# Two transformer blocks on one core: block 2's tokens in the order of residues mod 16

## The chip, the cores and the metric

The kernel runs on one core of a Trainium2 chip. Its time is that of one launch in device microseconds (us). The engines are named as in the profile: PE is TensorE (matmul), PEld its weight load, DVE VectorE, ACT ScalarE, POOL GpSimd, SP SyncE, which issues most of the DMAs. The kernel before took 2622.14 us, the median of three runs (2611.28 to 2628.56).

## The reference, cut to what matters

x has 2048 tokens of 1024 features. Block 1 (gated spatial mixing, a 31-wide convolution, windowed attention, an output projection with layer norm) gives x1. Block 2 works on x1:

```python
h = rmsnorm(x, norm_pre_g); z = h @ w_in
q, k, v, g_attn, c_h, c_b, c_c, g_conv = split(z)      # q, k, v: 12 heads of 64
q, k = rope(q, pos), rope(k, pos)
for window, dilation in ((128, 1), (512, 4), (2048, 16)):
    # query s sees the keys s, s-d, s-2d, ..., s-window: positions regrouped by
    # residue mod d, then a causal window of 128 keys inside each residue
    o_i, lse_i = dilated_window_attn(q, k, v, window, dilation)
mix_w = softmax(stack(lses)); o = sum(mix_w * outs)    # three patterns mixed per query and head
attn_out = o * silu(g_attn)
conv_out = c_b * causal_depthwise_conv(c_c * c_h, conv_w) * silu(g_conv)   # 3 taps: s, s-1, s-2
x = x + rmsnorm(concat(attn_out, conv_out) @ w_out, norm_post_g)
```

All of it is float32. The kernel forms products from a high and a low part of each operand (three matmuls in the dense projections, L163).

## The kernel before, in words

Block 2 runs in stages: `norm_stage` (x1 rows in from DRAM, normed, transposed, values of all heads), `rope_stage` (q and k), `gate_stage` (gates and convolution), then `dilated_stage`, and in it, after the attention, the output projection. Intermediate tensors go through DRAM (`scr_...`): `q2h`, `q2l`, `k2h`, `k2l` are the high and low parts of q and k, features by tokens; `v23` the values, tokens by heads; `sg2` the gate. `project_stage` before them writes x1, 128 rows at a time (L1325, the last block L1237); `norm_stage` loads it four blocks at a time (L304), each of the first four after the store of just that block.

**Attention.** Heads go in pairs j = 0 to 5. For each pair there are three patterns d = 1, 4, 16 (16, 4, 1 for the last pair), each of 16 units of 128 queries. Unit g is block b of residue r. It sees its own block of 128 keys and the one before it in the same residue (nk = 2, w = 256), or its own alone where there is none before (nk = 1): one unit in d=1, four in d=4, all 16 in d=16. Queries and keys are read from SBUF with stride d.

One unit passes these steps; in the list `work` step s holds scores of unit s, turn and rest of unit s-4, exps of unit s-1, gather of unit s-6, and every engine follows the list in its order:
- scores (PE, L1779 and L1780): for each of the two heads, q's high and low halves (64 + 64 rows) against k's high part twice, and the same against k's low part with zeros in the other half (buffers lA and lB, cleared by POOL once, L1948); both heads in one PSUM bank;
- mask and row maximum (DVE, L1845), exponentials (ACT, L1824);
- turn (PE, L1790): transposes, which ACT (L1817) and DVE (L1851) split into high and low;
- gather (PE, L1808): probabilities times values, ten small matmuls for each key block;
- rows out of PSUM every second unit (DVE L1857 or ACT L1830), into `kept` (d=1) or `ob` (others). Every four units `ob` goes to DRAM (`scr_part`, L1926).

**Mix.** When a pair's third pattern is done, four mixes begin, one for each quarter of the tokens, each in parts A to G on consecutive steps: A (SP, L1936) fetches the two stored patterns' rows into `cm`, and the gate; B (DVE, L1868) is the first use of `cm`; C an exponential (ACT); D, F and G are POOL's (L1731 to L1758), E DVE's. A stands four steps before B; the four A stand 9 steps apart. There are two `cm` buffers, so the third A waits for the first mix's G. SP works through its list in order too: it also holds the loads of the next pair's q and k (L1897 to L1901, ten DMAs of 512 KB, one every second step from unit 8 of d=1 on), the values of the next pattern (L1909, L1913, at unit 6), the part stores. The first pair's q and k come in four chunks of ten DMAs each, and a unit of the first pattern waits for its own chunk alone.

## Time and profile before

| | us |
|---|---|
| median of three runs | 2622.14 |
| profiled execution | 2614.59 |
| its span | 2612.8 |
| PE busy | 2393.4 |
| DVE busy | 1414.2 |
| ACT busy | 840.9 |
| POOL busy | 681.2 |
| share of L163 (dense projections) in the chain that ended last | 50% |

The span runs from the first to the last instruction; the profiled execution's time is 1.8 us more. A busy PE is not PE at its peak: matmuls are pipelined and overlap, so that the distance between the starts of two of them says more than the duration of one. The chain that ended last is followed back from the last instruction, at each step to what released it.

### The profile page before, as it was taken

Reading aid. Unit: us, or ns where it says so; the run is one execution under the profiler, and the core shown is the slowest. Engines: PE = TensorE matmul, PEld = TensorE weight load, DVE = VectorE, ACT = ScalarE, POOL = GpSimd, SP = SyncE. Lnnn points to the kernel's source line nnn. Section 1 sums busy time; section 2 is a strip of 40 time slices with the busy share of each in tenths; the row PEclk is TensorE's granted clock in tenths of the full one; section 3 lists DMA queues with packets and bytes.
Section 4 is the critical chain, followed back from the end, with each engine's and each line's share of the span. In section 5 each row is a group of like instructions: output and inputs, shape, how many; then the busy total and the mean of one; then the engine's idle time right before and its main releaser. Section 6 shows DMA issues by size and latency. Waiting matters only on the chain.

```text
span 2612.8 us, 47838 instructions
## 1 busy us (share of the span) xinstructions
PE 2393.4 (92%) x18958; PEld 2144.8 (82%) x18958; DVE 1414.2 (54%) x3441; ACT 840.9 (32%) x1938; POOL 681.2 (26%) x652
## 2 busy tenths in 40 slices
PE   6999899796999799699999999999699899897898
PEld 5977899796677688599888888889698899896777
DVE  6414768854798454663465533131476676675322
ACT  4411111111567110253122211011475676565111
POOL 0002011153231689200110111110105344443222
PEclk9999899898799899899999999999899999998999
DMA  4341320135640233332455531111858866964442
GB/s 148 113 104 55 102 72 23 58 99 154 178 114 22 101 121 109 121 126 94 143 188 164 175 98 65 49 61 49 200 150 194 204 171 165 203 196 153 147 140 103
DMA packets 283761, 322.19 MB, mean 123 GB/s; under 512 B 38049, under 2 KB 221217, under 8 KB 280081
## 3 DMA queue, kind: packets, MB, share of 16 engines
q1 hardware_dynamic: 281712, 313.09, 41.4%
q0 software_dynamic: 1680, 5.51, 0.7%
q8 instruction: 151, 2.47, 0.4%
q14 instruction: 74, 0.60, 0.1%
q10 hardware_dynamic: 144, 0.52, 0.0%
HBM read 196.91 MB, written 109.56 MB: 117 GB/s over the span
## 4 chain that ended last, share of the span: by engine, by line
PE 67%; DVE 10%; DMA 8%; issue 7%; POOL 3%; SPq 3%; ACT 2%; DVEq 0%; POOLq 0%; ACTq 0%
PE bank L163 50%; DMA cm<-scr_part 4%; PE bank L1779 3%; PE bank L1808 3%; DVE acc L642 3%; PE bank L1780 3%; PE bank L1790 3%; SPq L1899 1%; PE bank L1031 1%; PE bank L352 1%; DMA yn<-scr_y 1%; ACT bf L375 1%; POOL yo L2057 1%; PE bank L1023 1%; DVE bst L312 1%
## 5 line engine op out<-in xcount | busy, mean ns | idle before, releaser
L163 PE MATMUL bank<-w1h,xh 128*128 128x256 f32 (+1 forms) x896 | 260.7, 291 | 15.1 <-DVE s1st L632 15.1
L163 PE MATMUL bank<-w1l,xh 128*128 128x256 f32 (+1 forms) x896 | 256.5, 286 | 0.0
L163 PE MATMUL bank<-w1h,xl 128*128 128x256 f32 (+1 forms) x896 | 256.3, 286 | 0.0
L163 PE MATMUL bank<-xh,w2h 128*128 128x512 f32 x640 | 249.0, 389 | 0.0
L163 PE MATMUL bank<-xl,w2h 128*128 128x512 f32 x640 | 249.0, 389 | 0.0
L163 PE MATMUL bank<-xh,w2l 128*128 128x512 f32 x640 | 249.0, 389 | 0.0
L163 PE MATMUL bank<-w2h,xh 128*128 128x256 f32 x768 | 220.4, 287 | 10.9 <-issue 6.5
L1845 DVE CUSTOM_DVE_ANT_0 s2m<-bank,mask 128x256 f32<-128x256 f32 (+1 forms) x576 | 186.6, 362 | 72.0 <-PE bank L1780 68.4
L163 PE MATMUL bank<-w2h,xl 128*128 128x256 f32 x768 | 219.7, 286 | 0.0
L163 PE MATMUL bank<-w2l,xh 128*128 128x256 f32 x768 | 219.6, 286 | 0.0
L642 DVE SCALAR_TENSOR_TENSOR acc<-ain,cw,acc 128x512 f32<-128x512 f32 x240 | 200.3, 836 | 8.9 <-ACT acc L599 1.8
L163 PEld LDWEIGHTS bank<-w1h,xh 128*128 128x128 f32 x896 | 176.5, 197 | 18.6 <-issue 17.6
L1851 DVE SCALAR_TENSOR_TENSOR p2l<-bank,p2h 128x512 f16<-128x512 f32 (+1 forms) x288 | 165.1, 573 | 46.9 <-ACT p2h L1817 35.6
L1817 ACT ACTIVATE p2h<-bank 128x512 f16<-128x512 f32 (+1 forms) x288 | 144.8, 503 | 128.1 <-PE bank L1790 126.2
L1790 PE MATMUL bank<-ident,p2r 128*128 128x128 f32 x900 | 154.8, 284 | 31.7 <-DVE p2l L1851 31.7
L163 PEld LDWEIGHTS bank<-w1l,xh 128*128 128x128 f32 x896 | 176.4, 197 | 1.6 <-issue 0.6
L163 PEld LDWEIGHTS bank<-w1h,xl 128*128 128x128 f32 x896 | 176.0, 196 | 0.0
L1808 PE MATMUL bank<-v,p2h 128*128 128x64 bf16 (+1 forms) x2700 | 169.2, 194 | 0.8 <-issue 0.5
L1808 PEld LDWEIGHTS bank<-v,p2h 128*128 128x128 f16 x2700 | 160.3, 98 | 4.3 <-issue 0.4
L163 PEld LDWEIGHTS bank<-w2h,xh 128*128 128x128 f32 x768 | 149.6, 195 | 12.0 <-issue 6.7
L1808 PE MATMUL bank<-v,p2l 128*128 128x64 bf16 (+1 forms) x1800 | 158.8, 194 | 0.0
L213 POOL CAST w2h<-w2r 128x2048 fp32r<-128x2048 f32 x13 | 24.6, 1895 | 509.5 <-DMA w2r<-in_w_in 411.0
(256 smaller groups left out, 6215.6 us busy)
## 6 DMA issues: line engine op xcount, KB each, us to landing
v<-scr_v SPq DMA_DIRECT2D x12, 1552.0 KB, 9.7
scr_part<-ob SPq DMA_DIRECT2D x48, 264.0 KB, 3.2
cm<-scr_part SPq DMA_DIRECT2D x48, 264.0 KB, 4.6
w2r<-in_w_in SPq DMA_DIRECT2D x12, 1024.0 KB, 6.2
qr<-qf SPq DMA_DIRECT2D x192, 64.0 KB, 2.0
scr_v<-bvo SPq DMA_DIRECT2D x24, 388.0 KB, 2.5
v<-scr_v SPq DMA_DIRECT2D x24, 388.0 KB, 5.8
ax<-in_x SPq DMA_DIRECT2D x16, 512.0 KB, 6.3
```

Of the source, the lines that this page charges most:

```text
L163: ins = nc.tensor.matmul(dst, x, y, start=k == 0 and m == 0, stop=k == n - 1 and m == 2)
L312: nc.vector.bn_stats(st[:, t, 6 * h:6 * h + 6], xs[t][:, 512 * h:512 * h + 512]).then_inc(*d_st.up())
L352: ins = nc.tensor.transpose(bank[:, 128 * t:128 * t + 128], xs[t][:, 128 * k:128 * k + 128], ident[:])
L375: nc.scalar.activation(xf[m % 2][:], bank[:], ACT.Identity, scale=gain[:, k:k + 1], **bias).then_inc(*a_turn.up())
L642: nc.vector.scalar_tensor_tensor(acc[:, cols], ain[:, 512 * q + m:512 * q + m + 512], cw[:, c, m:m + 1], acc[:, cols], ALU.mult, ALU.add). ...
L1779: nc.tensor.matmul(dst, buf[hh][:, qc], buf[2 + hh][:, kc], start=True, stop=False)
L1780: ins = nc.tensor.matmul(dst, buf[hh][:, qc], buf[4 + hh][:, kc], start=False, stop=True)
L1790: ins = nc.tensor.transpose(bank[:, w * hh + 128 * c:w * hh + 128 * c + 128], p[:, hh, 128 * c:128 * c + 128], ident[:])
L1808: ins = nc.tensor.matmul(bank[:, c0:c0 + n], a[:, pc], vt[:, x["v0"] + c, vc], start=c == 0 and m == 0, stop=c == nk - 1 and m == 4)
L1817: nc.scalar.activation(pth[u % 3][:, 0:2 * x["w"]], x["t"][0][:, 0:2 * x["w"]], ACT.Copy, scale=PSCALE).then_inc(*a_ph.up())
L1845: nc.vector.tensor_tensor_reduce(sm[u % 3][:, hh, 0:w], x["s"][0][:, 256 * hh:256 * hh + w], mask2[:, 256 - w:256], 1.0, -NEG, ALU.add, AL ...
L1851: nc.vector.scalar_tensor_tensor(ptl[u % 3][:, 0:w], x["t"][0][:, 0:w], PSCALE, pth[u % 3][:, 0:w], ALU.mult, ALU.subtract).then_inc(*d_pl ...
```

## The change

Block 2 takes its tokens in the order of residues mod 16: position 128 r + l holds token 16 l + r. x1 is stored so, and every later tensor of block 2 has this order; the output rows go back to their places at the last store. In it the keys of a d=16 unit are 128 neighbours; those of a d=4 block are 4 runs of 32; those of a d=1 block 16 runs of 8 (`blocks`). Inside a unit, queries, keys, values and mask have the order of these runs.

- x1's row blocks are stored as 8 x 16 rows (`x1_rows`), and block 2's first load waits for all of them.
- Rope reads cos and sin with a stride of 16. The convolution's taps are 128 columns apart, with one more small copy on DVE.
- The patterns' order is 16, 4, 1 (1, 4, 16 for the last pair). `kept` holds d=16; d=4 and d=1 go to DRAM.
- For d=4 and d=1 POOL copies the queries of four units at a time into `qd` (item "reorder", one copy per head, 128x512), 6 to 8 steps ahead.
- k's low part has one buffer: head 0 in rows 0 to 63, head 1 in rows 64 to 127. The matmul with it takes 64 rows. The zero fills go.
- Two units are scored at once, each head in a bank of its own. Of each unit: high of both heads, then low of both.
- Values and parts move by residue: 1 DMA for d=16, 4 for d=4, 16 for d=1 (`STRIPES`, 8 d partitions each). A pattern's rows are stored in one go when all 16 units are done.
- Masks for d=4 and d=1 are loaded by 4 and 16 DMAs at the stage's start and reordered by DVE.
- A mix's A stands 9 steps before its B, and the four A 7 steps apart, the first 3 steps later than before.

```diff
+STRIPES = {1: 16, 4: 4, 16: 1}
...
-                elif x_ready is not None:
-                    sp.wait_ge(*x_ready[t])
+                elif t == 0:
+                    for token in x_ready:
+                        sp.wait_ge(*token)
...
+        def x1_rows(n):
+
+            return x1.rearrange("(r t l) c -> t l r c", r=16, t=NT)[n]
...
-        return [(x_out[t], x_out[t].base + 16) for t in range(4)]
+        return [s.now() for s in (*x_out, x_last)]
...
-                c, q, r = x["c"], qf[m % 3], qr[m % 2]
+                q, r = (b[:].rearrange("p (r l) -> p r l", r=4) for b in (qf[m % 3], qr[m % 2]))
+                cos, sin = (b[:].rearrange("p (l r) -> p r l", r=16)[:, 4 * x["g"]:4 * x["g"] + 4, :] for b in (cosT, sinT))
                 dve.wait_ge(*a_q.at(m + 1))
                 dve.wait_ge(*r_in[m % 2].at(64 * (m // 2 + 1)))
                 dve.wait_ge(*c_in.at(32))
-                nc.vector.tensor_tensor(q[:], q[:], cosT[:, c:c + 512], ALU.mult).then_inc(*d_rp.up())
-                nc.vector.tensor_tensor(r[:], r[:], sinT[:, c:c + 512], ALU.mult).then_inc(*d_rp.up())
+                nc.vector.tensor_tensor(q, q, cos, ALU.mult).then_inc(*d_rp.up())
...
+                        nc.vector.tensor_copy(uin[:, 0:2, 1:128], uin[:, 16:18, 0:127]).then_inc(*d_z.up())
...
+        part_rows = sbs("prow", 2, [128, NT, PW], F32, late_scope)
...
-        qk = [[sb(f"qk{n}{i}", [128, S], FR, scope) for n in ("qA", "qB", "kA", "kB", "lA", "lB")] for i in range(2)]
+        qk = [[sb(f"qk{n}{i}", [128, S], FR, scope) for n in ("qA", "qB", "kA", "kB", "l")] for i in range(2)]
+        qd = [sbs(f"qd{i}", 2, [128, 4, 128], FR, scope) for i in range(3)]
         vr = sbs("v2", 2, [128, 16, 2 * VW], BF, scope)
-        ob = sbs("ob", 4, [128, 4, PW], F32, scope)
         sm, pr = sbs("s2m", 3, [128, 2, 256], F32, scope), sbs("p2r", 4, [128, 2, 256], F32, scope)
         pth, ptl = sbs("p2h", 3, [128, 512], FH, scope), sbs("p2l", 3, [128, 512], FH, scope)
-        mask2 = sb("mask2", [128, 256], scope=scope)
-
-        m_in, qk_in, q0_in, v_in, o_out = sem("ld0"), sems("qk", 2), sems("qk0", 4), sems("v2", 2), sems("ob", 4)
+        mask = {d: sb(f"mask{d}", [128, 256], scope=scope) for d in PATTERNS}
...
-        pairs = [(j, d) for j in range(6) for d in (PATTERNS if j < 5 else PATTERNS[::-1])]
+        d_mx, d_pl, d_row, d_min, d_rec, d_mix, d_mask = (sem("d_" + n) for n in ("mx", "pl", "row", "min", "rec", "mix", "mask"))
+        g_q, g_mix = sem("g_q"), sem("g_mix")
+
+        ORDER = PATTERNS[::-1]
+        pairs = [(j, d) for j in range(6) for d in (ORDER if j < 5 else ORDER[::-1])]
...
+        fours = [u for u in range(0, N, 4) if units[u]["d"] < 16]
+        for n, u in enumerate(fours):
+            for x in units[u:u + 4]:
+                x["of4"] = n
...
-            mixing.append([t, [None] * delay + ["A"] + [None] * (3 if j < 5 else 0) + list("BCDEFG")])
+            mixing.append([t, [None] * delay + ["A"] + [None] * (8 if j < 5 else 0) + list("BCDEFG")])
...
-                if g == 15 and d == 16 and j < 5:
+                if g == 15 and d == 1 and j < 5:
                     for quarter in range(4):
-                        mix(j, quarter, quarter == 3, 9 * quarter, "pool", work)
-                if j == 5 and d == 1 and g % 4 == 3:
+                        mix(j, quarter, quarter == 3, 3 + 7 * quarter, "pool", work)
+                if j == 5 and d == 16 and g % 4 == 3:
...
+            if s % 2 == 0 and s - s % 4 + 8 in fours:
+                work.append(("reorder", s - s % 4 + 8, s % 4 // 2))
+            if g == 7 and d == 16:
                 loading = [("pair", j + 1, 1, k) for k in range(10)] if j + 1 < 6 else []
             if (j, d, g) == (5, 4, 0):
                 work += [("weights", 0), ("weights", 1)]
-            if (g + 16 * PATTERNS.index(d) if d < 16 else 0) >= 8 and g % 2 == 0 and loading:
+            if (g + 16 * ORDER.index(d) if d > 1 else 0) >= 8 and g % 2 == 0 and loading:
                 work.append(loading.pop(0))
...
-                x["s"] = sbk.take(d_mx.at(2 * item[1] + 2))
-                if x["d"] > 1:
-                    if x["g"] % 4 == 0:
-                        n_ob += 1
+
+                u = item[1]
+                x["s"] = [banks[u // 2 % 2 * 2 + hh][:, 256 * (u % 2):256 * (u % 2) + x["w"]] for hh in range(2)]
+                x["s_before"] = s_before if u < 4 else [d_mx.at(2 * (u - 4) + 4)]
...
+        def blocks(x, d):
+
+            return x.rearrange("p (r t l) -> p t r l", t=NT, l=8 * d)
+
+        def stripes(x, d):
+
+            return x.rearrange("(r t l) c -> r l t c", t=NT, l=8 * d)
...
-            if item[0] == "scores":
-                u, x = item[1], units[item[1]]
-                j, d, w, buf = x["j"], x["d"], x["w"], qk[x["j"] % 2]
-                bank, before = x["s"]
+            if item[0] == "scores" and item[1] % 2 == 0:
+                two = units[item[1]:item[1] + 2]
+                x = two[1]
+                j, d, buf = x["j"], x["d"], qk[x["j"] % 2]
                 if j == 0:
-                    for c in range(x["g"] // 4 + 1 if d == 1 else 4):
+                    for c in range(x["g"] // 4 + 1 if d == 16 else 4):
                         pe.wait_ge(*q0_in[c].at(160))
                 else:
                     pe.wait_ge(*qk_in[j % 2].at(160 * ((j + 1) // 2)))
-                pe.wait_ge(*g_zero.at(4))
-                pe.wait_ge(*before)
-                q0, k0 = x["r"] + d * 128 * x["b"], x["r"] + d * 128 * (x["b"] - x["nk"] + 1)
-                qc, kc = slice(q0, q0 + d * 127 + 1, d), slice(k0, k0 + d * (w - 1) + 1, d)
-                for hh in range(2):
-                    dst = bank[:, 256 * hh:256 * hh + w]
-                    nc.tensor.matmul(dst, buf[hh][:, qc], buf[2 + hh][:, kc], start=True, stop=False)
-                    ins = nc.tensor.matmul(dst, buf[hh][:, qc], buf[4 + hh][:, kc], start=False, stop=True)
-                ins.then_inc(*p_s.up())
+                if d < 16:
+                    pe.wait_ge(*g_q.at(2 * (x["of4"] + 1)))
+                for before in two[0]["s_before"]:
+                    pe.wait_ge(*before)
+                for x in two:
+                    for second in (False, True):
+                        for hh in range(2):
+                            g, k0 = x["g"], x["g"] - x["nk"] + 1
+                            dst = x["s"][hh].rearrange("p (t r l) -> p t r l", t=x["nk"], l=8 * d)
+                            q = buf[hh][:, 128 * g:128 * g + 128] if d == 16 else qd[x["of4"] % 3][hh][:, g % 4, :]
+                            own = slice(64 * hh, 64 * hh + 64)
+                            if second:
+                                ins = nc.tensor.matmul(dst, q[own], blocks(buf[4][:], d)[own, k0:g + 1], start=False, stop=True)
+                            else:
+                                nc.tensor.matmul(dst, q, blocks(buf[2 + hh][:], d)[:, k0:g + 1], start=True, stop=False)
+                ins.then_inc(*p_s.up(2))
...
+            if item[0] == "reorder":
+                _, u, hh = item
+                x = units[u]
+                j, d, g, n = x["j"], x["d"], x["g"], x["of4"]
+                if n >= 3:
+                    pool.wait_ge(*p_s.at(fours[n - 3] + 4))
+                for token in [q.at(160) for q in q0_in] if j == 0 else [qk_in[j % 2].at(160 * ((j + 1) // 2))]:
+                    pool.wait_ge(*token)
+                nc.gpsimd.tensor_copy(qd[n % 3][hh][:].rearrange("p t (r l) -> p t r l", l=8 * d), blocks(qk[j % 2][hh][:], d)[:, g:g + 4]).then_inc(*g_q.up())
...
-                nb, c = NT // d, 2 * VW * j
+                c = 2 * VW * j
                 if n >= 2:
                     sp.wait_ge(*p_o.at(16 * (n - 1)))
-                if d == 16:
-                    nc.sync.dma_start(vr[n % 2][:], v23.rearrange("(p r) c -> p r c", r=16)[:, :, c:c + 2 * VW]).then_inc(*v_in[n % 2].up(16))
-                else:
-                    view = v23.rearrange("(b p r) c -> r p b c", p=128, r=d)
-                    for r in range(d):
-                        nc.sync.dma_start(vr[n % 2][:, r * nb:r * nb + nb, :], view[r][:, :, c:c + 2 * VW]).then_inc(*v_in[n % 2].up(16))
+                for r in range(STRIPES[d]):
+                    nc.sync.dma_start(vr[n % 2][8 * d * r:8 * d * r + 8 * d, :, :], stripes(v23[:, c:c + 2 * VW], d)[r]).then_inc(*v_in[n % 2].up(16))
...
-                if g % 4 == 3 and d > 1:
-                    p = part[PATTERNS.index(d) - 1][j]
-                    dst = (p.rearrange("(b p r) c -> r p b c", p=128, r=4)[g // 4] if d == 4 else
-                           p.rearrange("(p r) c -> p r c", r=16)[:, g - 3:g + 1, :])
+                if g == 15 and d < 16:
                     for token in x["rows"]:
                         sp.wait_ge(*token)
                     sp.wait_ge(*d_mx.at(2 * u + 2))
-                    nc.sync.dma_start(dst, ob[x["ob"] % 4][:]).then_inc(*o_out[x["ob"] % 4].up(16))
+                    for r in range(STRIPES[d]):
+                        nc.sync.dma_start(stripes(part[d][j], d)[r], out_of(x)[8 * d * r:8 * d * r + 8 * d, :, :]).then_inc(*o_out[x["ob"] % 2].up(16))
...
-                for i in range(4):
-                    sp.wait_ge(*o_out[i].at(16 * (2 * j + 2)))
+                for token in parts_at[j]:
+                    sp.wait_ge(*token)
                 if k >= 2:
                     sp.wait_ge(*after[mix_order[k - 2], "G"])
-                for n in range(2):
-                    nc.sync.dma_start(cm[slot][:, :, n, :], part[n][j][rows, :].rearrange("(t p) c -> p t c", p=128)).then_inc(*cm_in[slot].up(16))
+                for n, d in enumerate((4, 1)):
+                    nc.sync.dma_start(cm[slot][:, :, n, :], part[d][j][rows, :].rearrange("(t p) c -> p t c", p=128)).then_inc(*cm_in[slot].up(16))
...
-        def pool_zeros():
-            for buf in qk:
-                for hh in range(2):
-                    nc.gpsimd.memset(f(buf[4 + hh][64 - 64 * hh:128 - 64 * hh, :]), 0.0).then_inc(*g_zero.up())
-
-        nc.sync.dma_start(mask2[:], A["c_mask2"]).then_inc(*m_in.up(16))
-        pool_zeros()
+
+        nc.sync.dma_start(mask[16][:], A["c_mask2"]).then_inc(*m_in.up(16))
+        for d in (4, 1):
+            for r in range(STRIPES[d]):
+                nc.sync.dma_start(sm[d // 4][8 * d * r:8 * d * r + 8 * d, 0, :], A["c_mask2"].rearrange("(l r) k -> r l k", r=STRIPES[d])[r]).then_inc(*m_in.up(16))
+        dve.wait_ge(*m_in.at(16 * 21))
+        for d in (4, 1):
+            nc.vector.tensor_copy(mask[d][:].rearrange("p (t r l) -> p t r l", t=2, l=8 * d),
+                                  sm[d // 4][:, 0, :].rearrange("p (t l r) -> p t r l", t=2, l=8 * d)).then_inc(*d_mask.up())
...
-                    nc.sync.dma_start(out_dst[128 * n:128 * n + 128, :], ybuf[n % 3][:]).then_inc(*o2_out[n % 3].up(16))
+                    nc.sync.dma_start(out_dst.rearrange("(l r) c -> r l c", r=16)[n], ybuf[n % 3][:]).then_inc(*o2_out[n % 3].up(16))
...
```

## Rows read from the trace of the kernel before

**Rows 1.** The page's chain that ended last: shares by engine, then by line.

```profile
PE 67%; DVE 10%; DMA 8%; issue 7%; POOL 3%; SPq 3%; ACT 2%; DVEq 0%; POOLq 0%; ACTq 0%
PE bank L163 50%; DMA cm<-scr_part 4%; PE bank L1779 3%; PE bank L1808 3%; DVE acc L642 3%; PE bank L1780 3%; PE bank L1790 3%; SPq L1899 1%; PE bank L1031 1%; PE bank L352 1%; DMA yn<-scr_y 1%; ACT bf L375 1%; POOL yo L2057 1%; PE bank L1023 1%; DVE bst L312 1%
```

**Rows 2.** By stretch: length, busy PE PEld DVE ACT POOL (instructions), clock, DMA share, GB/s.

```profile
2031.00:2120.00 89.00, 82.13 (x1092) 80.31 (x1091) 61.86 (x269) 59.47 (x157) 39.62 (x76) 0.98 0.78 187
...
2210.00:2302.00 92.00, 84.82 (x1093) 83.22 (x1091) 62.54 (x272) 59.35 (x156) 39.65 (x76) 0.94 0.76 181
2302.00:2385.00 83.00, 76.81 (x1081) 75.21 (x1080) 64.92 (x259) 58.23 (x152) 49.59 (x95) 1.00 0.58 169
```

**Rows 3.** Timeline of PE, a d=1 unit: start us, us, instruction.

```profile
2034.33 0.36 PE L1779 MATMUL bank<-qkkA,qkqA 128*128 128x256 f32 x1
2034.54 0.28 PE L1780 MATMUL bank<-qklA,qkqA 128*128 128x256 f32 x1
...
2034.89 0.60 PE L1790 MATMUL bank<-ident,p2r 128*128 128x128 f32 x4
...
2035.93 0.36 PE L1779 MATMUL bank<-qkkA,qkqA 128*128 128x256 f32 x1
```

**Rows 4.** Timeline of PE, scores of a d=4 unit.

```profile
1973.84 0.58 PE L1779 MATMUL bank<-qkkA,qkqA 128*128 128x256 f32 x1
...
1974.96 0.29 PE L1790 MATMUL bank<-ident,p2r 128*128 128x128 f32 x1
```

**Rows 5.** Timeline of PE, scores of a d=16 unit.

```profile
2103.83 0.44 PE L1779 MATMUL bank<-qkkA,qkqA 128*128 128x128 f32 x1
...
2104.74 0.40 PE L1790 MATMUL bank<-ident,p2r 128*128 128x128 f32 x2
```

**Rows 6.** Timeline of PE in the window stage of block 1.

```profile
700.49 0.42 PE L1022 MATMUL bank<-kTA,qTA 128*128 128x384 f32 x1
700.83 0.44 PE L1023 MATMUL bank<-kTl,qTA 64*128 64x384 f32 x1
701.20 0.55 PE L1031 MATMUL bank<-ident,pr 128*128 128x128 f32 x3
```

**Rows 7.** Waits, 1853 to 2302 us: total, times, longest.

```profile
DVE ce L1868 <- DMA cm<-scr_part: 51.1, 12, 8.5
...
PE bank L1790 <- DVE p2l L1851: 26.4, 10, 5.7
```

**Rows 8.** Timeline of PE at the start of the attention, idle before in brackets.

```profile
1859.27 0.58 PE L1779 MATMUL bank<-qkkA,qkqA 128*128 128x256 f32 x1 [10.34 <-DMA qklB<-scr_k2l]
```

**Rows 9.** Timeline at the last x1 store (DVE, ACT) and at attention's start (SP).

```profile
1073.67 1.28 DVE L312 BATCH_NORM_STATS2 bst<-bx 128x6 f32<-128x512 f32 x2
...
1073.79 0.34 ACTq L1237 DMA_DIRECT2D scr_x<-xr  x1
...
1835.65 0.35 SPq L1950 DMA_DIRECT2D mask<-in_c_mask  x1
...
1836.06 0.49 SPq L1899 DMA_DIRECT2D qkqA<-scr_q2h  x1
```

**Rows 10.** DMA issues: KB each, median us from issue to landing.

```profile
v<-scr_v SPq DMA_DIRECT2D x12, 1552.0 KB, 9.7
...
cm<-scr_part SPq DMA_DIRECT2D x48, 264.0 KB, 4.6
...
bx<-scr_x SPq DMA_DIRECT2D x16, 512.0 KB, 5.8
...
scr_x<-xr SPq DMA_DIRECT2D x15, 512.0 KB, 3.0
```

**Rows 11.** POOL's instructions by line: busy us, mean ns.

```profile
L1750 POOL TENSOR_TENSOR cm<-cm,cd 128x512 f32<-128x512 f32 x42 | 43.0, 1045 | 0.0
...
L1754 POOL TENSOR_TENSOR kept<-kept,cm 128x512 f32<-128x512 f32 x21 | 27.1, 1288 | 1.6
...
L213 POOL CAST w2h<-w2r 128x2048 fp32r<-128x2048 f32 x13 | 24.6, 1895 | 509.5 <-DMA w2r<-in_w_in 411.0 <-PE bank L163 49.3 <-DMA qr<-qf 49.1
```

75 lines of the change are left out of this document (44 added, 31 removed).

## The prediction

> **What bounds the kernel now.** I read the page's chain first, then the busy time by stretches, then the instructions one by one. The chain [rows 1] is two thirds TensorE; half is the dense projections (L163), which the change leaves alone but for the order of the tokens. What changes lies in block 2's dilated attention, 1836 to about 2385 us. I cut it by head pair (48 units each; the five with mixes are like one another but for the last): 89 to 92 us per pair, in which TensorE is busy 82 to 85, DVE 62, ACT 59, POOL 40, and the DMA engines 0.76 to 0.78 of the time, so about 69 us of full DMA work per pair [rows 2]. TensorE is the bound, DMA close behind. The last pair loads nothing for a next one: 83 us, DMA at 0.58.
>
> What TensorE does in one unit of two key blocks with d=1: scores from 2034.33 to 2034.89, 0.56 us; turning and gathering last until 2035.93: 1.60 together [rows 3]. With d=4 the same four score matmuls take 1.12 (1973.84 to 1974.96) [rows 4], and with d=16, where a unit has 128 keys, 0.91 [rows 5]. So the reader sees the strides: half the columns with d=16 cost 1.6 times as much as d=1. A pair is 16 d=1 units (one of them with one key block), 16 d=4 (four with one), 16 d=16 (all with one).
>
> The second loss is waits. Between 1853 and 2302 DVE waited 51.1 us in 12 places for the mix's data from DRAM (cm), and TensorE in its turn 26.4 us for DVE [rows 7], some 6.6 per pair with mixes.
>
> **The change part by part.**
>
> Scores. The keys become runs of 8 or 32 elements, d=16 queries a plain block, others are copied by POOL: the strides go. But the low part becomes a 64-row matmul where it was a 128-row one with zeros, and the order in a unit is high, high, low, low: two switches of row shape per unit. What a switch costs is seen in the window stage, whose scores are built so: the 128-row matmul of 384 columns starts at 700.49, the 64-row one at 700.83, the next 128-row one at 701.20 [rows 6], steps of 0.34 and 0.37, where [rows 3] has 0.12 (2034.54 to 2034.89 in three) for 256 columns without a switch. The rows leave 0.21 between first and second matmul after a gather (a weight load laid bare, 0.10 above that pitch). My unit of two key blocks: 0.21 (high to high) + 0.19 (0.34 less that 0.10, less 0.05 for 128 fewer columns) + 0.05 (second low, between nothing, if the two run beside each other on their own rows, and 0.11) + 0.32 (0.37 less 0.05) = 0.77 us; with one key block 0.10 less, 0.67. Bounds: 0.45 if no switch costs anything and the lows overlap (0.56 less 0.11); 0.93 if every step costs as in [rows 6].
>
> The Trainium skill (TensorEngine Tiling (Array Packing), Key Properties) says both that different tiles can load and multiply in parallel and that changing the tiling mode drains the TensorE. By its first sentence alone the unit would be at my lower bound; the second is what [rows 6] show, and I go by the row.
>
> Per pair: d=1 15 x (+0.21) + 0.11 = +3.3; d=4 12 x (0.77 - 1.12) = -4.2, 4 x (0.67 - 0.91) = -1.0; d=16 16 x (0.67 - 0.91) = -3.8. Sum -5.7, six pairs -34. In the first pair the gain of the first pattern is not had: its 16 units wait for their four chunks of q and k (TensorE idle 10.34 us before 1859.27 [rows 8]; ten issues of 0.6 us per chunk), +4. So **-30**.
>
> Scoring two units at once only changes who waits within two units: both engines behind have spare time (DVE 62, ACT 59 of about 77 [rows 2]). Nothing.
>
> Later mixes. From the issue of cm to its first use there are 9 steps instead of 4, at 1.6 us about 14 us instead of 7, against 4.6 us landing when quiet [rows 10]. But cm still queues behind the loads of the next pair and now behind 16 value loads and 16 part stores on SP; a part store is also only issued when its pattern is done. And the third mix's fetch waits for the first one's G (7 us of POOL: three products of 1.05, three further operations of 1.29 [rows 11]) in SP's order, with the values of d=1 and three q/k loads queued behind it, then the fourth mix's fetch. I leave 3 of the 6.6 us: four pairs x 3.6 = **-14**. Bounds: -26 (all gone), +15 (as much lost again at the fourth mix).
>
> POOL gets 96 copies of 128x512. Between a quarter of the 2048-wide cast (0.47) and a two-input operation (1.29) [rows 11]; I take 0.7: 11 us a pair on top of 40, hidden by TensorE's 77. They stand 6 to 8 units ahead, about 10 us, and G's 7 us can stand before them: no stall, little room. Upper bound 1 us a pair.
>
> DMA issues. SP issues 63 in a pair against 36; the smallest cost 0.35 each [rows 9]. 22 us of SP's time is hidden. Not hidden: at the stage's start 20 small mask loads go ahead of the first q load, which now is issued at 1836.06, right after one mask load of 0.35 to 0.41 [rows 9]. 20 x 0.4 = **+8**, nothing covers it, for TensorE waits for exactly these loads. The two mask reorderings on DVE lie under the same wait. The four zero fills on POOL go, hidden before.
>
> x1. Block 2's first four loads (512 KB each) needed only the first four row blocks and had landed before the last was stored; now they need all rows. The last store is issued at 1073.79 [rows 9], lands 3.0 later, the first load 5.8 after that [rows 10]: the statistics of the norm, which began at 1073.67 [rows 9], begin at about 1082.6. TensorE waits for them: **+9** (7 to 13).
>
> Rope with strided cos/sin, one small copy per convolution half, output rows 64 KB apart in DRAM: rope and gates stand in the chain with the projections' L163 [rows 1], DVE beside it; output rows stay 4 KB pieces. Nothing. If that cover were gone: 96 strided rope operations, at 0.1 us more each 10 us.
>
> The last pair has no loads for a following one; its mixes still use their data at once. Nothing.
>
> Sum: -30 - 14 + 8 + 9 = **-27**. The profiled execution took 2614.6 us (span 2612.8), so 2588; the median of three is 7.5 above it. Between the two scales I say 2590.
>
> **The rivals.**
>
> A. The switches cost little, the low matmuls run side by side: 0.45 per unit. Then TensorE loses 19.5 us a pair (d=1 16 x 0.11, d=4 12 x 0.67 + 4 x 0.48, d=16 16 x 0.48 with 0.43 for one block) and has about 63 and no longer bounds; DMA does, with 69 us of work [rows 2]. At some 75 us per pair instead of 89: four pairs x -14.5, -8 in the last, -4 in the first, -70, +17 for the starts: -53, 2562. For it: the two lows go to different rows and banks. Against it: [rows 6]. 0.25.
>
> B. Slower: the d=1 values and parts move as 16 pieces of 8 partitions. If such a piece keeps only 8 of the 16 DMA engines busy, those eight carry 1.55 MB of values [rows 10] and 1.08 MB of parts (2048 rows of 528 bytes) twice as long. A pair moves 187 GB/s x 89 us = 16.6 MB in 69 us of DMA work [rows 2], 4.2 us a MB: 69 + 11 = 80 us on the busier half, more than TensorE's 77 (82.7 - 5.7). cm, values and q/k of the next pair then land late, each before an engine that stops for it: 10 us in each of five pairs, -27 + 50 = +23, 2638. It decides where these eight engines need more than the pair's TensorE time. No row has a transfer of fewer than 32 partitions to judge by, so 0.16.
>
> The Trainium skill (DMA: Bandwidth & Descriptors, Why a DMA increments its semaphore by 16 and not by 1) says the number of engines is the largest up to 16 that divides both sides' slowest dimension: 8 here. No row here shows it; it speaks for B, and for 2 us more at x1.
>
> C. It doesn't pay: the switch from high to low costs 0.29, the 0.10 of [rows 6] not taken off: 0.87 per unit, +0.10 x 48 = +4.8 a pair, +27 in all: 0, 2614 to 2622. At 0.93 it is +17, 2632 to 2639. 0.14.
>
> The forecast's own case 0.45, 2565 to 2605.
>
> **How the numbers follow.** This kernel's measurement tells about 1% (26 us) from no change; the forecast lies right on it. Faster by over 1%: 0.27 of the forecast's 0.45 and all of A: 0.52. Within: 0.18, and 0.12 of C: 0.30. Slower: B and the rest, 0.18. The range 2550 to 2635 leaves out a tenth at A's end (copies and waits all hidden) and a tenth at B's.
>
> **What would show it.** In the profile after: the steps of the score matmuls in one d=1 unit (0.77 us for four; 0.45 would be A, 0.87 C); weight loads of q shorter than now; idle before 64-row matmuls put to "issue"; DVE's wait for cm under 25 us; POOL's copies near 0.7; the first score matmul some 8 us later after the last gate store; 9 us more between the last x1 store and the first transpose; time from issue to landing of the d=1 values and the DMA share per pair (B). Wrong if a pair takes under 73 or over 88 us.

## The result and the profile after

| | us | |
|---|---|---|
| before, median of 4 beside it | 2620.1 | 2611.3 to 2628.6 |
| changed, median of 4 | 2767.5 | 2759.2 to 2775.2 |
| ratio | 1.0562 | [1.0512, 1.0613] |
| profiled execution, span (mean clock) | 2760.7 (0.917) | before: 2612.8 (0.956) |

147 us slower where 27 us faster was forecast. The chain of waits of the changed kernel, shares by engine and by line:

```profile
PE 61%; DMA 11%; DVE 9%; issue 8%; SPq 5%; POOL 4%; ACT 2%; DVEq 0%; POOLq 0%; ACTq 0%
PE bank L164 48%; DMA cm<-scr_part 6%; DVE acc L644 3%; PE bank L1857 3%; PE bank L1839 3%; SPq L1978 2%; PE bank L1829 2%; PE bank L1827 1%; DMA scr_part<-prow 1%; PE bank L1033 1%; PE bank L354 1%; ACT bf L377 1%; PE bank L1025 1%; SPq L1957 1%; SPq L1988 1%
```

Against [rows 1] TensorE's share falls from 67% to 61%, and DMA rises from 8% to 11%, SP's queue from 3% to 5%; the line of the part stores (L1978) is new in it. The projections (L164 now) are the same work. I date each part of the attention by its first unit's eviction of p2l, 48 units to a pair:

| us | first p2l | pair 1 | 2 | 3 | 4 | 5 | 6 | from last p2l to the end |
|---|---|---|---|---|---|---|---|---|
| before | 1861.4 | 81.3 | 88.3 | 89.3 | 90.3 | 91.6 | 80.5 | 230.0 |
| changed | 1876.8 | 92.1 | 116.6 | 119.5 | 115.3 | 114.5 | 98.2 | 227.9 |

So 15.4 us are lost ahead of the attention, 134.7 in it, and 2.2 come back behind it. These are dates of one execution each: in the kernels of e1, e3, e4, e6, e10 and e13, which change nothing ahead of the attention, the first p2l comes anywhere from 1875.7 to 1884.9. The busy time in three of these pairs (columns in the first line, as in [rows 2]):

```profile
core 0: us, PE busy (x) PEld busy (x) DVE busy (x) ACT busy (x) POOL busy (x), PEclk, DMA share, GB/s
1968.90:2085.40 116.50, 85.91 (x1096) 72.68 (x1093) 62.52 (x268) 58.40 (x157) 48.78 (x92) 0.81 0.76 143
2085.40:2204.90 119.50, 84.58 (x1099) 71.52 (x1096) 62.33 (x268) 58.47 (x158) 48.62 (x92) 0.81 0.75 139
...
2434.70:2532.90 98.20, 79.67 (x1074) 68.38 (x1071) 62.03 (x254) 56.59 (x152) 54.18 (x103) 0.85 0.60 149
```

TensorE is busy for 86 us of 116.5, and so idle for 30; before it was busy for 82 of 89. It is busy for longer although the strides are gone: its clock is 0.81 where [rows 2] have 0.98 to 0.94. (The clock has two levels, 1.00 is 2.4 GHz and 0.50 is 1.2 GHz; a value between is the mean of a stretch.) Two stretches, the first inside an idle stretch of TensorE, the second right behind it:

```profile
1991.00:1998.00 7.00, 0.00 (x0) 0.00 (x0) 1.09 (x7) 0.11 (x1) 0.67 (x4) 0.50 1.19 220
1999.00:2007.00 8.00, 8.00 (x72) 6.92 (x71) 5.81 (x24) 4.92 (x13) 7.00 (x12) 0.50 1.03 200
```

TensorE stands idle for over 9 us eight times in the four middle pairs. Each time the clock goes to its lower level during the idle stretch and stays there past its end. The bytes are the same (143 GB/s x 116.5 us = 16.7 MB), but the DMA engines work 0.76 x 116.5 = 88 us on them, not 69. (The share adds up the times of all packets over 16 engines; packets overlap, so it can come out above 1.) The waits (total us, times, longest) say what TensorE stands idle for:

```profile
DVE ce L1917 <- DMA cm<-scr_part: 156.8, 16, 21.5
...
PE bank L1839 <- DVE p2l L1900: 95.8, 18, 13.5
...
PE bank L1857 <- issue: 46.3, 5, 13.0
```

DVE's wait for the mix's data is 156.8 us; before it was 58.1 up to the stage's end (51.1 of it in the stretch of [rows 7]), and its longest grew from 8.5 to 21.5. DVE's evictions queue behind it, and TensorE's wait for them went from 31.7 (26.4 of it in [rows 7]) to 95.8. The 46.3 us ahead of the gathers (L1857), put to "issue", are waits for the values: in the four middle pairs TensorE stands 9.3 to 13.0 us ahead of the gather of the first d=1 unit, and where the values come in one DMA (e2, below) 0.6 is left. Yet TensorE's own pace is as forecast. Timeline of PE, the scores of two d=1 units (start, us, instruction):

```profile
2069.01 0.38 PE L1829 MATMUL bank<-qkkA,qd 128*128 128x256 f32 x1
2069.22 0.30 PE L1829 MATMUL bank<-qkkB,qd 128*128 128x256 f32 x1
2069.45 0.40 PE L1827 MATMUL bank<-qkl,qd 64*128 64x256 f32 x2
2069.79 0.40 PE L1829 MATMUL bank<-qkkA,qd 128*128 128x256 f32 x1
2070.02 0.30 PE L1829 MATMUL bank<-qkkB,qd 128*128 128x256 f32 x1
2070.25 0.40 PE L1827 MATMUL bank<-qkl,qd 64*128 64x256 f32 x2
2070.58 0.66 PE L1839 MATMUL bank<-ident,p2r 128*128 128x128 f32 x4
```

Eight score matmuls take 2069.01 to 2070.58: 0.785 us a unit, forecast 0.77. The two low matmuls, one row "x2", share 0.40 us: their two records start within 0.01 us of each other and take 0.40 each, so they run side by side. What went wrong stands in the timeline of SP's queue (start, time that the issues took, tensor, count):

```profile
1970.59 11.58 SPq L1978 DMA_DIRECT2D scr_part<-prow  x16
1982.21 2.70 SPq L1967 DMA_DIRECT2D v<-scr_v  x4
1985.34 3.19 SPq L1988 DMA_DIRECT2D cm<-scr_part  x2
...
2008.70 0.92 SPq L1988 DMA_DIRECT2D cm<-scr_part  x2
2019.97 0.36 SPq L1991 DMA_DIRECT2D gt<-scr_sg  x1
2020.37 13.26 SPq L1967 DMA_DIRECT2D v<-scr_v  x16
2033.67 0.86 SPq L1957 DMA_DIRECT2D qkqB<-scr_q2h  x1
...
2035.85 3.34 SPq L1988 DMA_DIRECT2D cm<-scr_part  x2
```

Sixteen part stores take 11.6 us to issue, 0.72 each, sixteen values 13.3, 0.83 each. The first cm fetch stands behind the stores and four value loads of d=4; the fourth behind the sixteen values and three q/k loads. The place in the queue isn't all: the fourth fetch begins to be issued at 2035.85, and DVE's wait for it, 21 us, ends at 2058.8, 23 us later ([rows 10] has 4.6 from issue to landing).

### The profile page after: what moved, and what is told of

It is laid out like the page before. It is cut to its first block, busy times and chain, and to the rows that moved or that the text cites. A ratio compares the mean times of both kernels' runs of the same rounds, so it can differ in the third digit from the quotient of the medians.

```text
span 2760.7 us, 48109 instructions
## 1 busy us (share of the span) xinstructions
PE 2414.8 (87%) x18958; PEld 2095.6 (76%) x18958; DVE 1460.8 (53%) x3445; ACT 830.5 (30%) x1938; POOL 721.6 (26%) x744
## 4 chain that ended last, share of the span: by engine, by line
PE 61%; DMA 11%; DVE 9%; issue 8%; SPq 5%; POOL 4%; ACT 2%; DVEq 0%; POOLq 0%; ACTq 0%
PE bank L164 48%; DMA cm<-scr_part 6%; DVE acc L644 3%; PE bank L1857 3%; PE bank L1839 3%; SPq L1978 2%; PE bank L1829 2%; PE bank L1827 1%; DMA scr_part<-prow 1%; PE bank L1033 1%; PE bank L354 1%; ACT bf L377 1%; PE bank L1025 1%; SPq L1957 1%; SPq L1988 1%
## 5 line engine op out<-in xcount | busy, mean ns | idle before, releaser
L164 PE MATMUL bank<-w1h,xh 128*128 128x256 f32 (+1 forms) x896 | 260.2, 290 | 14.9 <-DVE s1st L634 14.9
L1839 PE MATMUL bank<-ident,p2r 128*128 128x128 f32 x900 | 180.9, 318 | 99.9 <-DVE p2l L1900 95.8
L164 PE MATMUL bank<-w1l,xh 128*128 128x256 f32 (+1 forms) x896 | 256.2, 286 | 0.0
L164 PE MATMUL bank<-w1h,xl 128*128 128x256 f32 (+1 forms) x896 | 256.1, 286 | 0.0
L164 PE MATMUL bank<-xh,w2h 128*128 128x512 f32 x640 | 249.0, 389 | 0.0
L164 PE MATMUL bank<-xl,w2h 128*128 128x512 f32 x640 | 249.0, 389 | 0.0
L164 PE MATMUL bank<-xh,w2l 128*128 128x512 f32 x640 | 249.0, 389 | 0.0
L1857 PE MATMUL bank<-v,p2h 128*128 128x64 bf16 (+1 forms) x2700 | 188.7, 204 | 46.3 <-issue 46.3
L164 PE MATMUL bank<-w2h,xh 128*128 128x256 f32 x768 | 220.5, 287 | 9.7 <-issue 6.4
L164 PE MATMUL bank<-w2l,xh 128*128 128x256 f32 x768 | 219.7, 286 | 0.0
L164 PE MATMUL bank<-w2h,xl 128*128 128x256 f32 x768 | 219.6, 286 | 0.0
L1857 PEld LDWEIGHTS bank<-v,p2h 128*128 128x128 f16 x2700 | 177.3, 106 | 53.6 <-issue 47.2
L1839 PEld LDWEIGHTS bank<-ident,p2r 128*128 128x128 f32 x900 | 106.6, 157 | 119.8 <-DVE p2l L1900 98.5
L164 PEld LDWEIGHTS bank<-w1h,xh 128*128 128x128 f32 x896 | 176.3, 197 | 18.4 <-issue 17.4
L164 PEld LDWEIGHTS bank<-w1l,xh 128*128 128x128 f32 x896 | 175.9, 196 | 1.6 <-issue 0.6
L1857 PE MATMUL bank<-v,p2l 128*128 128x64 bf16 (+1 forms) x1800 | 176.2, 203 | 0.0
L164 PEld LDWEIGHTS bank<-w1h,xl 128*128 128x128 f32 x896 | 175.8, 196 | 0.0
L1873 ACT ACTIVATE p2r<-s2m,prow 128x256 f32<-128x256 f32 (+1 forms) x384 | 165.9, 483 | 0.0
```

Source lines behind the costliest of these rows:

```text
L164: ins = nc.tensor.matmul(dst, x, y, start=k == 0 and m == 0, stop=k == n - 1 and m == 2)
L1839: ins = nc.tensor.transpose(bank[:, w * hh + 128 * c:w * hh + 128 * c + 128], p[:, hh, 128 * c:128 * c + 128], ident[:])
L1857: ins = nc.tensor.matmul(bank[:, c0:c0 + n], a[:, pc], vt[:, x["v0"] + c, vc], start=c == 0 and m == 0, stop=c == nk - 1 and m == 4)
L1873: nc.scalar.activation(pr[u % 4][:, hh, 0:w], sm[u % 3][:, hh, 0:w], ACT.Exp, bias=row[:, 130 + hh:131 + hh], scale=-1.0).then_inc(*a_ex.up())
```

## The experiments

The theories. **Pieces**: the 16 small DMAs of d=1 cost the time, through the engines that they keep busy (rival B) or through SP's time and order. **Switches**: the row switches cost TensorE more than the strides did. **Mix places**: the later mixes lose time rather than win it. **Gate**: a gate fetch that waits in SP's queue for a slot's y store holds back what stands behind it. In the expectations "theory S" is the width of the pieces, "theory I" the issues, "theory Q" SP held by the mix's own waits, for a free cm buffer and for the gate's store. All ratios are to the kernel before on the same chip; a difference between two kernels is the difference of their ratios times 2618.

### e1, e13: the same sixteen DMAs, other partitions

```diff
-    for r in range(16): dma(vr[8*r:8*r+8, :, :], stripes(v, 1)[r])         # 8 partitions x 16 tiles
+    for t in range(16): dma(vr[:, t, :], v.rearrange("(r t l) c -> t r l c", t=16, l=8)[t])   # e1: 128 partitions x 1 tile
+    for r in range(16): dma(vr[16*(r//2):16*(r//2)+16, 8*(r%2):8*(r%2)+8, :], plain(v)[same])  # e13: 16 partitions x 8 tiles
```

(The part stores alike. e13 moves plain rows, so it attends to other tokens; only its time counts.)

> The changed kernel, but the values and parts of d=1 still move in 16 DMAs, each now over all 128 partitions (one tile of 128 rows) instead of 8 partitions and 16 tiles; same bytes, same pieces of 776 and 528 bytes, same number of issues. Theory S (pieces of 8 partitions load only part of the DMA engines, so the transfers take longer and all behind them is late): the mix's wait for cm falls from 151 us to under 70, the kernel comes to 2640 to 2700. Theory I (the price is the 16 issues in SP's order, 11 to 13 us each time): nothing changes in the issues, 2750 to 2780. Theory Q (SP is held by the mix's own waits for a free buffer and for the gate store): 2740 to 2780.

e1: 2699.0 us (2686.8 to 2705.0), 1.0308 [1.0268, 1.0349]. Its waits:

```profile
DVE ce L1917 <- DMA cm<-scr_part: 97.9, 16, 11.5
...
PE bank L1839 <- DVE p2l L1900: 87.9, 17, 10.5
```

The waits fell with the time, though not under the 70 us that theory S wanted: 66 us (0.0254) come from the form of the pieces at the same number of them. e1 changes the number of partitions from 8 to 128, though, and could win by the span of partitions or by the number of engines. e13 tells these apart.

> The changed kernel, with the values and the stored parts of d=1 again in 16 DMAs each, but each of 16 partitions by 8 tiles and not of 8 partitions by 16 tiles (plain rows, so other tokens are attended to; bytes, number of issues and their places are the same). If the number of DMA engines that serve a piece of 8 partitions is what made the changed kernel dearer than e1_spread (rival B's mechanism): near e1_spread, 2690 to 2715 us, and the waits of the mixes for cm near e1's 98 us. If it is that a piece covers few partitions: near the changed kernel, 2745 to 2775 us, and those waits near 151 us.

e13: 2700.2 us (2694.0 to 2701.6), 1.0306 [1.0278, 1.0334]. For the kernel's time pieces of 16 partitions are as good as pieces of 128, and both 66 to 67 us better than pieces of 8. Stretches in which the part stores, then the values, move (last columns: DMA share, GB/s), first of the changed kernel, then of e13 with one of its pairs, then of e1:

```profile
1972.00:1984.00 12.00, 12.00 (x168) 10.34 (x165) 10.51 (x56) 9.12 (x32) 0.00 (x0) 1.00 0.45 90
2024.00:2032.00 8.00, 6.33 (x56) 4.91 (x54) 4.40 (x17) 4.12 (x11) 6.53 (x19) 0.79 0.62 99
```

```profile
1973.00:1981.00 8.00, 8.00 (x120) 7.07 (x119) 6.89 (x39) 6.22 (x21) 0.00 (x0) 1.00 0.75 126
2020.00:2027.00 7.00, 7.00 (x92) 5.78 (x90) 4.83 (x20) 4.48 (x12) 5.95 (x9) 0.89 1.06 134
2072.50:2170.70 98.20, 82.30 (x1099) 69.37 (x1096) 62.23 (x268) 58.33 (x158) 48.60 (x92) 0.88 0.85 169
```

```profile
1974.00:1985.00 11.00, 11.00 (x157) 9.61 (x154) 9.61 (x54) 8.59 (x29) 0.00 (x0) 1.00 0.37 94
2026.00:2035.00 9.00, 7.34 (x103) 5.83 (x102) 6.22 (x26) 5.52 (x15) 7.44 (x19) 1.00 0.70 190
```

While the stores move, the share is 0.45 in the changed kernel, with 8-partition pieces, and 0.75 with 16; while the values move 0.62 (a y store moves beside them) and 1.06. The share alone doesn't tell how many engines a piece uses: e1, with all 128 partitions, has 0.37 and 0.70. The DMA packets in the trace do. In the changed kernel 8 to 11 value packets (776 bytes) are under way at once for nine tenths of 2022 to 2032; in e13 it is 16 or more for over three quarters of 2020 to 2027. e13's pair takes 98.2 us instead of 119.5. The sixteen issues of e13, then of e1 (0.51 and 0.54 us each in e13, 0.69 in e1, where the changed kernel has 0.72 and 0.83):

```profile
1972.28 8.20 SPq L1984 DMA_DIRECT2D scr_part<-prow  x16
...
2018.48 8.62 SPq L1968 DMA_DIRECT2D v<-scr_v  x16
```

```profile
1973.36 10.97 SPq L1983 DMA_DIRECT2D scr_part<-prow  x16
...
2024.81 10.99 SPq L1968 DMA_DIRECT2D v<-scr_v  x16
```

So SP's long issues are not simply the engines' backlog: e1's take 0.69 us each while the DMA share is 0.37. What makes an issue long stays open. Rival B's mechanism is shown: an 8-partition piece keeps half of the 16 engines busy. With the rule of the Trainium skill that the prediction quoted (DMA: Bandwidth & Descriptors, Why a DMA increments its semaphore by 16 and not by 1), 8 engines at 8 partitions and 16 at 16, the trace agrees: 8 to 11 packets under way against 16 and more.

A second cost lies in few partitions with many tiles. Over the attention the median packet of 776 bytes takes 62 ns in the changed kernel and 65 in e13, but 38 in e1, in e2 and in the kernel before. So the DMA work of a pair grows (88 us; e13 0.85 x 98.2 = 83) also where all 16 engines serve a piece. e13's transfers are slower than e1's and its issues shorter, so the two equal times may be a balance of both; no run parts them.

### e2, e6, e7: no pieces at all

```diff
-    for r in range(16): dma(vr[8*r:8*r+8], stripes(v, d)[r])
+    dma(vr[:], v.rearrange("(t p) c -> p t c", p=128))        # e2, e6; part stores alike in e2 alone
-    matmul(dst, q[own], k_low[own])                            # e7: e2 and this
+    matmul(dst, q, k_low)
```

> The changed kernel, but every pattern's values and parts move in one DMA each, rows in plain order (so the values and parts of d=4 and d=1 are of other tokens than they should be; times alone are of use). 1 issue instead of 16 and 4. Theory S and I both: a large fall; what it gains over the run with 16 DMAs of 128 partitions is the price of the issues. S alone: like that run, 2640 to 2700. I alone: 2620 to 2660, while that run stays near 2767. Theory Q: still over 2700, since the third mix's fetch still holds SP.

(e2, e6 and e7 read other tokens' rows, and e7 also adds products that don't belong; only their times count.)

e2: 2621.6 us (2617.5 to 2629.0), 1.0021 [1.0006, 1.0037]. Its waits and two of its pairs:

```profile
DVE ce L1917 <- DMA cm<-scr_part: 35.7, 12, 7.0
...
PE bank L1839 <- DVE p2l L1900: 32.1, 12, 5.9
```

```profile
2048.00:2130.00 82.00, 79.06 (x1097) 66.92 (x1094) 62.42 (x269) 57.95 (x157) 48.78 (x92) 0.94 0.85 203
2130.00:2214.30 84.30, 78.17 (x1097) 66.05 (x1094) 61.85 (x268) 58.23 (x157) 48.65 (x92) 0.96 0.84 197
```

142 us (0.0541) came from the form of the values' and parts' transfers and nothing else: bytes, tensors, waits and places in the queue are the same. e2 also makes one DMA of the four pieces of d=4; no run parts these from the sixteen of d=1. The clock is back at 0.94 and 0.96 with TensorE fed, and its busy time per pair falls from 86 to 79 us. So what the rest of the change wins it also loses.

> The changed kernel with its values in one DMA per pattern, rows in plain order (values of d=4 and d=1 are of other tokens; times alone are of use); parts still in 4 and 16 pieces. Both in one DMA each came to 2622, none to 2767. If the values are the dearer part (they stand between the third and the fourth mix's fetch): 2665 to 2690. If the parts are (the first mix's fetch waits for their landing): 2700 to 2735.

e6: 2653.2 us (2651.3 to 2667.2), 1.0146 [1.0104, 1.0188]. It came below both ranges expected. The values carry 109 us of the 142, the stores 33. The values stand just ahead of the q/k loads and the fourth mix's fetch.

> The run with one DMA for each pattern's values and parts (2622 us, other tokens' rows), and the low matmul over all 128 rows (products of a low q part with the other head's low k part are added). With the waits gone TensorE's pace should decide more than in the changed kernel, where the 128 rows brought 31 us: 2575 to 2590. If the DMA engines bound it, under 15 us: 2607 to 2622.

e7: 2595.8 us (2587.0 to 2602.9), 0.9911 [0.9875, 0.9946], the fastest of all, but no version to use. It came between the two ranges expected. The 64-row form costs 0.0110, 29 us give or take 10, where the pieces are not in the way.

### e3: the low part without the row switch

```diff
-    matmul(dst, q[own], k_low[own], start=False)      # 64 rows
+    matmul(dst, q, k_low, start=False)                # 128 rows
```

> The changed kernel, but the matmul with k's low part takes all 128 rows (it adds products of the other head that don't belong; times alone are of use): no switch of row shape. The scores of two units should take about 1.1 us instead of 1.57 when nothing else waits. If TensorE's pace sets the time, some 0.2 us x 288 = 60 us less, 2700 to 2715; if the waits for data do, under 20 us, 2745 to 2770.

e3: 2736.3 us (2732.4 to 2740.4), 1.0457 [1.0427, 1.0487]: 27 us less than the changed kernel, between the two ranges expected, though DVE waits longer for cm (176.1, where it was 156.8). The switches are real and small: 27 us, give or take some 15, of a loss of 147 plus a missed gain of 27.

### e4: the mixes at their old places

```diff
-  ["A"] + [None] * (8 if j < 5 else 0)      mix(..., 3 + 7 * quarter, ...)
+  ["A"] + [None] * (3 if j < 5 else 0)      mix(..., 9 * quarter, ...)
```

> The changed kernel with the mixes' old places: A 4 steps before B and 9 steps apart, first A at once. If the later mixes help as meant, 20 to 50 us more than 2767. Theory Q (the buffer wait that the new places bring, third A before the first mix's G is done, holds SP with the values behind it): equal or less, 2720 to 2770.

e4: 2794.9 us (2785.4 to 2796.3), 1.0683 [1.0649, 1.0717]. The later mixes help, by 32 us: the rival that they hurt falls.

### e5: the pieces spread over the steps

```diff
+    if 6 <= g < 14: work += two ("value", n + 1, t)            # instead of 16 in a row
-    if g == 15: 16 part stores
+    if g % 2 == 1: the part stores of the two units just done   # pieces as in e1
```

> The run with 16 DMAs of 128 partitions for d=1's values and parts (2699 us), but spread in SP's order: two value loads on each of eight steps instead of sixteen in one step, two part stores after every second unit instead of sixteen when the pattern is done. Same DMAs, same sizes, same number. If what remains of the loss is that 16 issues in a row stand before the mix's fetch and the next loads (theory I, order): 2620 to 2655, DVE's wait for cm under 60 us. If it is the number of DMAs as such (each takes its time on the engines or in SP wherever it stands): 2680 to 2705.

e5: 2660.5 us (2656.5 to 2663.8), 1.0162 [1.0127, 1.0197]: 38 us less than e1 with the same DMAs. DVE's wait for cm is 47.1 us, its longest 6.0 instead of 11.5. The time lies between its two cases. What is left to e2 is 37 us: the number of DMAs, that of d=4 with it, and their places. TensorE still waits 20.5 us ahead of the gathers, for values that now come step by step (e2: 0.6), so not all of the 37 is the number itself.

### e8, e9, e12, e14: a better version of the change

```diff
e8:  e5 + e3's 128-row low + the masks as three plain loads behind the first q/k chunk
e9:  e8 + gate fetch (gt) moved on SP from the mix's part A to its part B
e12: e9 + mix starts 3 + 9 * quarter (were 3 + 7 * quarter)
e14: e9 + the d=1 value loads on ACT's queue (were on SP's)
```

> Spread issues, low matmul over all 128 rows, and the three masks as three plain loads behind the first chunk of q and k instead of 21 DMAs ahead of it. The terms as they stand: the run with spread issues less 30 us (rows), less 8 (masks): 2580 to 2620, at best 1% under the kernel before. If SP's issues as such are the price, 2640 to 2665.

e8: 2618.3 us (2610.6 to 2621.4), 0.9998 [0.998, 1.0017]: no gain over the kernel before. With the 128-row low matmul e8 and the three built on it add to each score the product of q's low part with the other head's low k part, which the reference doesn't have.

> The same move of the gate's fetch on the run with spread issues, 128-row low matmul and plain masks (2618 us). Its SP stood 12.6 us between the third mix's cm and gate fetch. If values and q/k behind it come earlier for it: 2585 to 2605. If the DMA engines (share 0.84 over a pair) are the bound by now: 2610 to 2620.

e9: 2610.8 us (2608.2 to 2619.1), 0.9973 [0.9959, 0.9987]: 7 us under e8, no more than the two intervals can tell. One of its pairs:

```profile
2040.80:2124.50 83.70, 71.73 (x1099) 69.88 (x1095) 61.94 (x269) 57.77 (x157) 48.61 (x92) 0.90 0.91 198
```

TensorE needs 72 us and the pair takes 84, with the DMA engines at 0.91. They are nearer to a bound than TensorE is, but no run shows that they are the bound: TensorE's waits for DVE still add up to 52.0 us.

> As the one before, and the mixes' four starts 9 steps apart instead of 7, so that the third fetch finds its cm buffer free (or nearly). If SP's hold there (some 7 us a pair) counts: 10 to 20 us less than with 7 steps. If the last mix, now 6 steps later, collides with the next pair's loads instead: equal or up to 15 more.

e12: 2633.2 us (2630.1 to 2640.7), 1.0061 [1.0041, 1.0081]: 23 us worse than e9 (at most 15 were expected), with DVE's wait for cm at 78.6 us. Mixes further apart don't help. Its waits show where they hurt: TensorE stands 21.9 us ahead of the gathers (4.3 in e9), and DVE waits 24.7 us for POOL's last step of a mix.

> e9_gate with the value loads of d=1 issued from ACT's queue, at the same steps, and no longer from SP. If SP's time for issues is still what holds the mixes' fetches: 2595 to 2606 us, and DVE's wait for cm falls from 38.5 to under 20 us. If the transfers' own time is: 2608 to 2620 us with that wait as it is. A third case: ACT's issues (some 0.7 us each, 16 per pair, by the SP rows) delay its evictions and exps; then PE's wait for p2h and p2l rises and the time is 2620 to 2660 us.

e14: 2635.8 us (2630.7 to 2643.0), 1.0055 [1.0029, 1.0081]: 21 us worse than e9. Waits of e9, then of e14 (TensorE's wait for DVE goes from 52.0 to 59.3):

```profile
DVE p2l L1902 <- ACT p2h L1868: 68.9, 78, 6.9
...
DVE ce L1919 <- DMA cm<-scr_part: 38.5, 11, 6.3
```

```profile
DVE p2l L1908 <- ACT p2h L1868: 93.6, 87, 10.1
...
DVE ce L1925 <- DMA cm<-scr_part: 38.1, 11, 6.0
```

The wait for cm doesn't move when SP is freed of 16 issues a pair: SP's time is no longer what holds the mixes back. ACT's evictions come later (93.6 against 68.9), the expectation's third case.

### e10: the gate fetch alone

> The changed kernel with one edit: the gate's fetch for a mix stands in SP's order beside part B instead of part A, nine steps later, when its buffer has long been stored. Theory Q (SP held about 10 us a pair by the wait for the gate store, the 16 value loads behind it): 30 to 50 us less than 2767. If that hold is only shifted to the next wait, under 15 us.

e10 (e9's move of the gate fetch, made on the changed kernel): 2788.4 us (2780.2 to 2800.4), 1.0653 [1.062, 1.0687], 24 us slower than the changed kernel, where both cases had it faster.

```profile
PE bank L1839 <- DVE p2l L1900: 162.8, 15, 24.6
...
POOL gt L1800 <- DMA gt<-scr_sg: 123.0, 9, 24.5
...
DVE ce L1917 <- DMA cm<-scr_part: 73.0, 11, 14.3
```

The wait for cm halves (from 156.8), and yet TensorE waits 162.8 for DVE, where it was 95.8: the wait only moved to a place where it hurts more. It is the same mechanism with another load: the second mix's gate fetch now stands behind the sixteen values (issued at 2035.34), POOL waits 123.0 us for the gate in nine places, ACT's exponential for POOL, and the evictions for ACT. So moving the gate fetch alone is no cure, and the total of one wait doesn't order two kernels.

### e11: the kernel before with the later mixes

e4's diff turned round, made on the kernel before, with e9's gate fetch.

> The kernel before (old order of tokens, strided keys) with two edits: A nine steps before B, starts 3, 10, 17, 24 steps after the pattern's end as in the changed kernel, and the gate's fetch beside B. If the later mixes were the useful part of the change: 20 to 30 us less than before, 2585 to 2600 (26 us of TensorE's waits are there to be had). If they only help where the DMAs are late: within 8 us of before.

e11: 2601.7 us (2599.1 to 2606.6), 0.9939 [0.9922, 0.9955]: the best version, faster than both kernels. Its waits, then a pair in the middle and the last:

```profile
PE bank L1790 <- DVE p2l L1851: 11.3, 5, 5.4
...
DVE ce L1868 <- DMA cm<-scr_part: 6.6, 2, 6.3
```

```profile
2033.60:2115.90 82.30, 81.30 (x1099) 79.85 (x1095) 63.04 (x271) 59.74 (x157) 39.76 (x76) 1.00 0.82 202
2281.00:2368.50 87.50, 78.37 (x1046) 76.77 (x1047) 63.77 (x255) 57.51 (x151) 49.61 (x95) 0.94 0.55 160
```

The wait for cm is 6.6 us (58.1 in the kernel before), and a pair takes 82.3 us with the clock at 1.00: TensorE is busy for 81.3 of it. The gain of 16 us lies between the two cases expected. It is that of the later places and of the gate fetch together.

## Why the prediction was wrong, step by step

**The step that failed** is the term DMA issues, which the sum put at nothing: "22 us of SP's time is hidden", at "the smallest cost 0.35 each". Measured were 0.72 and 0.83 us each, and they were not hidden. The next cm fetches stood in line behind them (DVE waited 156.8 us for cm, TensorE 95.8 for DVE), and the values themselves came late (46.3 us of TensorE's). I took the smallest price, counted the total, and never asked which load stands behind sixteen issues in a row; that the transfers themselves get slower was left to rival B. Of the 142 us that e2 gave back, 66 are the pieces' form (e1, e13), 38 their standing in a row (e5), 37 their number, with that of d=4 and what the spread places leave (e2 against e5), each give or take 10 to 17 by the intervals. These follow one another in that order; another order of the edits may divide the sum otherwise. Why such an issue takes 0.7 us and not 0.35 stays open.

**Rival B** had the mechanism right, and the chance (0.16) and price (+50) wrong. It counted 11 us more work for the busier half and 10 us per pair; the four middle pairs grew by 27 each (116.5 against 89.9 in the mean). The sum took DMA work at 4.2 us a MB; it was 88 / 16.7 = 5.3, for the single packets take longer as well, which "the busier half works longer" doesn't contain. That growth isn't what the 66 us bought: e13 has most of it (83 us of work a pair) and is as fast as e1. And rival B held one load late for one wait, where each late cm stops DVE, DVE stops TensorE, and TensorE then runs at a clock of 0.81: 86 us busy for what takes 79 in e2. That last step, what TensorE loses at the lower level of its clock, was nowhere in the prediction.

**Scores** (-30): the unit was right, 0.785 for 0.77. Rival C (0.87) and A (0.45) are out. Its worth shows only in e2, and only at the same clock: at 0.94 TensorE is busy for 79.1 us a pair where [rows 2] have 84.8, so -5.8 where -5.7 was forecast. The low matmul's switches cost 27 to 29 us of what the removed strides give.

**Later mixes** (-14, bounds -26 to +15): -32 in the changed kernel (e4), with the queue fuller; on the kernel before, together with the gate fetch, -16 (e11). My worry about the gate's slot isn't settled: SP does stand from the third cm fetch at 2008.70 to its gate fetch at 2019.97, but taking the gate fetch out of there made the changed kernel slower (e10), and where the issues are spread it brought 7 us that the intervals don't tell from none (e9).

**The last pair** (nothing but the scores' -5.7): wrong by 14 us. Without the pieces it takes 89.2 us (e2), in e11 87.5, before 80.5, while the middle ones take 84 and 83 instead of 90. In e11 the mixes' places and the gate fetch are the only edits, so these bring the longer last pair. In both kernels DVE waits there for POOL in a mix, 5.8 us in e11 and 6.9 in e2, where the kernel before has no such wait. The row of e2:

```profile
DVE ce L1922 <- POOL ce L1781: 6.9, 1, 6.9
```

**POOL's copies**: 0.61 us each for 0.7, hidden:

```profile
L1935 POOL CAST qd<-qkqB 128x512 fp32r<-128x512 f32 x48 | 29.4, 612 | 0.1
```

**Masks and x1** (+8, +9): block 2's first statistics begin at 1084.98 instead of 1073.67, 11.3 us later, as x1 said (7 to 13). The twenty small mask loads take SP 7.24 us, and the first q load is issued 18.0 us later than before (1854.06 against 1836.06), near the 17 of both terms. Rope, convolution and output: behind the attention 2.2 us fewer, nothing as forecast.

**The first pair** had another loss, which the prediction didn't have. Stretches of e2, then of the kernel before:

```profile
1880.00:1904.00 24.00, 24.00 (x184) 20.21 (x183) 12.77 (x67) 11.93 (x39) 3.40 (x6) 0.50 1.02 234
```

```profile
1863.00:1900.00 37.00, 37.00 (x539) 36.47 (x538) 28.89 (x106) 28.71 (x68) 0.00 (x0) 1.00 0.95 227
```

In e2 TensorE's clock stays at its lower level until 1904.9, 25 us after the first p2l, though TensorE is busy throughout; before, it is at the upper level from 1862.6 on, 1.2 us after it. The sixteen kernels fall into two groups. In the eight with the 64-row low matmul (the changed kernel, e1, e2, e4, e5, e6, e10, e13) the clock rises 24 to 34 us after the first p2l, in the eight with 128 rows (the kernel before, e3, e7, e8, e9, e11, e12, e14) 1 to 5 us after it. e3 differs from the changed kernel, and e7 from e2, in this alone, and their first pairs are 10 and 7 us shorter. So the row form costs TensorE its clock at this place, a good part of the 27 to 29 us; no run shows why.

The sign hung on one queue. With the d=1 and d=4 transfers of e2 the forecast's other terms come to +5 instead of -27 (ratio 1.0021). Of the 32 between them the last pair has 14 (8.7 longer where 5.7 shorter was expected), the four middle pairs 12 (83.7 us where 80.6 was expected, their DMA share being 0.84 and 0.85), the first some 5 (84.3 where 79.6 was expected), and the rest is ahead of the attention and behind it.
